# A hybrid decoder layer: the last four down-projection sums seeded into PSUM, two output tiles stored plainly, and a reordered scan

## The chip, the core and the metric

The kernel runs on one NeuronCore of a Trainium2 chip. The metric is the device time of one execution in microseconds (us); lower is better. The kernel before takes 1620.8 us (median of three runs, 1617.77 to 1620.87).

## What is computed

One decoder layer over 1024 tokens (plus 16 meta tokens) of width 1024, in float32:

```python
h = concatenate([meta_tokens, x])
mix = hybrid_mixer(rmsnorm(h, norm_mix_pre), ...)   # attention (8 heads) beside a Mamba-2 SSD scan, then @ w_out
h = h + rmsnorm(mix, norm_mix_post)
f = square(relu(rmsnorm(h, norm_mlp_pre) @ w_mlp_up)) @ w_mlp_down
h = h + rmsnorm(f, norm_mlp_post)
return h[:, N_META:]
```

The change touches three places: attention's transfers, the scan's order of work, and the last two lines, where `f` is normalised over its 1024 columns, weighted and added to the residual `h`.

## The kernel before, in words

Every matrix product is made of three passes in float32r, on operands cut into a high and a low part (high x high, high x low, low x high). The order of each engine's work is written out by hand, one function per engine and phase, with semaphores between them. An engine waits for a semaphore in its own order, so whatever is queued behind a waiting instruction waits too. `SP` (SyncE) issues nearly all transfers and computes nothing; accumulating transfers (`accum_op`) are issued by GpSimd.

**Attention** (`phase_attend`) works head after head. In `on_sync`, `head(h, ...)` issues for each head: the weights of head h+2, two "pieces" (`pieces(h, 0, 2)`), the rotated queries of head h+1 (`rotated`, four transfers, line 1469), a third piece, the first half of the head's output (`outputs(h, 0)`), the remaining pieces and the second half. A piece is a block of scan input that GpSimd weights and cuts in four parts; `store_piece` waits for GpSimd's two results, stores each as two parts (line 1488), and loads the piece after next (line 1481). GpSimd's next piece waits in turn for those stores. TensorE begins head h+1's scores at line 1722, behind a wait for the rotated queries (`a_qr_in`). Scan inputs and attention work share the time of this phase.

**The scan** (`phase_rest`, `chunk(t)` in each engine's function) works through eight chunks of 128 tokens. TensorE mixes the scan's own products with 16 blocks of the output projection, `attention(t, n0, n1)`, each three matmuls of 512 columns. Blocks 0 to 7 make one sum in PSUM bank 4, blocks 8 to 15 another in the same bank, so between block 7 and block 8 ScalarE has to copy the bank out (`mix_out(t, 0)`, line 2873) into `mixs`. TensorE's order in the middle of a chunk t of 1 to 5: blocks 5 and 6; `update(t)` (the state's product, line 2609); `diag(t, 1)` (line 2624); `decays(t, 3)` (lines 1343 and 1344); block 7; `diag(t, 2)`; a wait for the copy; blocks 8 to 11; `diag(t, 3)`; blocks 12 to 15. Chunk 0 has `update` later, and in chunk 6 the first eight blocks of chunk 7 stand before its own blocks 8 to 15. ScalarE's order there: exponentials 2 (`expo(t, 2)`, line 1359), `w_hi(t, 2)` (line 1370), `expo(t, 3)`, `mix_out(t, 0)`, `w_hi(t, 3)`. `expo(t, 3)` waits for `decays(t, 3)`.

**The MLP** runs in slices of 256 hidden columns. For each slice TensorE makes the up products (line 2784) and then 16 down products, two halves for each of eight row tiles, six matmuls of 512 columns each (line 2798; in the last slice line 2833, `down_last`). Each goes to PSUM, and VectorE adds it to the running sum `acc` in SBUF (line 3261, in the last slice `last_add`, line 3458, both halves of a tile in one instruction of 1024 columns). The order of tiles is `TILES`; i below is the place in it, 0 to 7. In the last slice tile i uses the two PSUM banks from `LAST_BANK[i % 4]`, so four tiles fill the eight banks and tile 4 takes the banks of tile 0.

**The end** makes, for each tile, a sum of squares on ScalarE (`last_square`, line 3072, 1024 columns of `acc`), one VectorE instruction (`last_v`, line 484), a square root on ScalarE (`last_sqrt`, line 3077) and five small VectorE instructions (`last_r`, lines 491 to 499), then the scaling by that number and by the weight row `e_wrow` (`last_scale`, line 3470, or, for tiles 2 and 6, ScalarE's line 3082 and GpSimd's multiplication, line 2550; for tile 7 two halves on VectorE, line 3498). `STATS_OF` says which tiles share one set of small instructions: 0; 1, 2; 3, 4; 5, 6; 7. The residual already stands in the output in HBM, and GpSimd issues accumulating stores onto it, one of 512 KB a tile (line 2554) and two of 256 KB for tile 7 (line 2558). SyncE's last wait is for all of them.

The lines that set the end's banks and order:

```python
TILES = [4, 5, 6, 7, 0, 1, 2, 3]
STATS_OF = ((0, 1), (1, 3), (3, 5), (5, 7), (7, 8))
BY_ACT = (2, 6)
LAST_BANK = (2, 4, 6, 0)
```

## Time and profile before

| | |
|---|---|
| median of three runs | 1620.8 us |
| the profiled execution, its own time | 1622.34 us |
| its span, first to last instruction | 1620.5 us |
| granted TensorE clock, mean of the span | 0.995 |
| TensorE busy | 1575.7 us (97%) |
| VectorE, ScalarE, GpSimd busy | 948.6, 599.4, 817.8 us |

The profiled execution is 1.84 us longer than its span and 1.5 us above the median. All places below are us from the start of the span. The phases in it: the input projection to about 360 us, attention to 665, the scan to about 841, the output projection's rest and the first norms to about 950, the MLP to 1602.5, and the end to 1620.5.

In a timeline row the first number is the start, the second the duration, and the bracket at the end is the engine's idle time before the row and what ended it. "x2" means that two instructions are merged in the row. In a window row each engine has its busy time and, in brackets, its count of instructions; then come the granted clock, the DMA engines' busy share and what they moved.

### The profile page before, as it was taken

How to read it: one execution, taken by the hardware profiler on the slowest of the kernel's cores; microseconds unless marked ns; L12 is line 12 of the kernel's file. 1: busy time of each engine (PE TensorE's matmuls, PEld its weight loads, DVE VectorE, ACT ScalarE, POOL GpSimd, SP SyncE). 2: the span in 40 equal slices, each digit the busy share in tenths (PEclk: the TensorE clock that was granted, in tenths of full speed). 3: DMA queues.
4: the chain of work that ended last, by engine and by line, in shares of the span. 5: the costliest groups of instructions: out<-in, count | busy, mean ns of one | idle time of the engine just before them, and what ended most of it. 6: DMA issues, size and time to landing. Idle time of an engine off the chain costs nothing.

```text
span 1620.5 us, 23514 instructions
## 1 busy us (share of the span) xinstructions
PE 1575.7 (97%) x8150; PEld 1353.1 (83%) x8150; DVE 948.6 (59%) x1582; ACT 599.4 (37%) x1149; POOL 817.8 (50%) x775
## 2 busy tenths in 40 slices
PE   7999999999999999899999999999999999999995
PEld 6999998878888888688887888888888888888884
DVE  4756525267677768577778668744444444444446
ACT  5222221245444544455554441433333323322223
POOL 7434453165776558642322340755555555555553
PEclk9999999999999999999999999999999999999998
DMA  6344512235556454788977720111111111111116
GB/s 209 108 139 126 160 56 69 65 109 175 166 147 185 127 155 146 272 312 286 333 245 263 266 79 27 52 52 52 52 52 51 49 50 51 52 52 52 51 46 104
DMA packets 180118, 204.22 MB, mean 126 GB/s; under 512 B 16328, under 2 KB 143152, under 8 KB 180048
## 3 DMA queue, kind: packets, MB, share of 16 engines
q1 hardware_dynamic: 178752, 199.12, 38.3%
q0 software_dynamic: 1296, 4.19, 1.6%
q8 instruction: 41, 0.67, 0.2%
q14 instruction: 29, 0.24, 0.0%
HBM read 133.96 MB, written 69.30 MB: 125 GB/s over the span
## 4 chain that ended last, share of the span: by engine, by line
PE 88%; DMA 3%; POOL 3%; DVE 3%; SPq 1%; issue 1%; ACT 1%; POOLq 0%; DVEq 0%; ACTq 0%
PE ps L2798 17%; PE ps L2784 17%; PE ps L793 7%; PE ps L852 6%; PE ps L2644 6%; PE ps L2719 4%; PE ps L1760 3%; PE ps L2750 3%; PE ps L2764 3%; PE ps L808 2%; PE ps L824 2%; PE ps L1746 2%; PE ps L1729 2%; PE ps L1677 1%; PE ps L2598 1%; PE ps L2833 1%
## 5 line engine op out<-in xcount | busy, mean ns | idle before, releaser
L3261 DVE TENSOR_TENSOR acc<-ps,acc 128x512 f32<-128x512 f32 x208 | 142.4, 690 | 114.8 <-PE ps L2798 114.8
L173 POOL TENSOR_TENSOR ring<-stage,zero 128x512 fp32r<-128x512 f32 (+2 forms) x83 | 91.2, 1099 | 190.9 <-DMA stage<-w_in 48.1
L2798 PE MATMUL ps<-wdlo,fshi 128*128 128x512 f32 x416 | 161.8, 389 | 0.0
L2798 PE MATMUL ps<-wdhi,fshi 128*128 128x512 f32 x416 | 161.8, 389 | 0.0
L2798 PE MATMUL ps<-wdhi,fslo 128*128 128x512 f32 x416 | 161.8, 389 | 0.0
L2534 POOL TENSOR_TENSOR wdlo<-wd_b,wdhi 128x512 fp32r<-128x512 f32 x56 | 70.7, 1293 | 141.4 <-ACT wdhi L3032 141.4
L3289 DVE TENSOR_TENSOR ps<-ps,fs_b 128x512 f32<-128x512 f32 x42 | 29.4, 699 | 150.6 <-PE ps L2784 150.6
L175 POOL TENSOR_TENSOR ring<-stage,ring 128x512 fp32r<-128x512 f32 (+2 forms) x83 | 109.6, 1321 | 6.5
L2644 PE MATMUL ps<-ring,s_aT 128*128 128x512 f32 x384 | 99.6, 403 | 5.9 <-DMA s_aT<-d_attlo 3.2
L793 PE MATMUL ps<-hThi,ring 128*128 128x346 f32 (+1 forms) x480 | 94.4, 325 | 0.0
L3027 ACT ACTIVATE fs_b<-ps 128x512 f32<-128x512 f32 x42 | 25.1, 597 | 184.1 <-PE ps L2784 184.1
L2798 PEld LDWEIGHTS ps<-wdhi,fshi 128*128 128x128 f32 x416 | 78.1, 188 | 16.4
L2798 PEld LDWEIGHTS ps<-wdhi,fslo 128*128 128x128 f32 x416 | 78.1, 188 | 16.2
L2798 PEld LDWEIGHTS ps<-wdlo,fshi 128*128 128x128 f32 x416 | 78.1, 188 | 16.1
L2644 PEld LDWEIGHTS ps<-ring,s_aT 128*128 128x128 f32 x384 | 71.3, 190 | 22.8 <-issue 4.1
L2719 PE MATMUL ps<-ring,s_aT 128*128 128x512 f32 x336 | 80.7, 397 | 1.0 <-DVE ring L3148 0.6
L852 PE MATMUL ps<-hThi,ring 128*128 128x512 f32 x256 | 80.4, 394 | 0.8 <-DVE dt L1119 0.8
L2506 POOL TENSOR_TENSOR wS_b<-wS_b,par 128x512 f32<-128x512 f32 x14 | 14.6, 1041 | 129.0 <-DMA wA_b<-w_mlp_up 129.0
L793 PEld LDWEIGHTS ps<-hThi,ring 128*128 128x128 f32 x480 | 78.7, 189 | 0.2
L2719 PEld LDWEIGHTS ps<-ring,s_aT 128*128 128x128 f32 x336 | 62.2, 188 | 16.4 <-DVE ring L3148 1.2
L2457 POOL TENSOR_TENSOR s_y<-s_y,s_off 128x512 f32<-128x512 f32 x16 | 21.2, 1322 | 103.0 <-DVE s_y L3119 103.0
L1854 ACT ACTIVATE pThi<-ps 128x512 fp32r<-128x512 f32 (+3 forms) x112 | 51.2, 506 | 31.8 <-PE ps L1746 31.8
(500 smaller groups left out, 4591.7 us busy)
## 6 DMA issues: line engine op xcount, KB each, us to landing
wd_b<-w_mlp_down SPq DMA_DIRECT2D x28, 512.0 KB, 3.9
wA_b<-w_mlp_up SPq DMA_DIRECT2D x42, 256.0 KB, 2.8
stage<-w_in SPq DMA_DIRECT2D x40, 256.0 KB, 2.7
stage<-w_out SPq DMA_DIRECT2D x28, 256.0 KB, 5.7
xt<-x SPq DMA_DIRECT2D x8, 512.0 KB, 7.3
d_xT<-xdT SPq DMA_DIRECT2D x8, 512.0 KB, 3.3
d_x<-x_tok SPq DMA_DIRECT2D x8, 512.0 KB, 4.6
d_zT<-zs SPq DMA_DIRECT2D x16, 256.0 KB, 2.3
```

What stands on the lines that cost most here:

```text
L173: pool.tensor_tensor(hi, src, k.zero[:, 0:1].broadcast_to([P, width]), ALU.add).then_inc(k.sem(fam + "_hi"), 1)
L175: pool.tensor_tensor(lo, src, hi.bitcast(F32), ALU.subtract).then_inc(k.sem(fam + "_cut"), 1)
L793: mm = pe.matmul(ps[:, base + q, 0:w], W[a][:, (8 * c + kk) % RING, P * j:P * j + P], hT[b][:, kk, c0:c0 + w], start=(kk == 0 and (a, b) = ...
L852: mm = pe.matmul(ps[:, g % 4, :], W[a][:, (8 * c + kk) % RING, P * j:P * j + P], hT[b][:, kk, c0:c0 + 512], start=(kk == 0 and (a, b) == ( ...
L1760: mm = pe.matmul(ps[:, bank, c0:512], v[a][:, u, vt, :], pT[b][:, j + 1, c0:512], start=(j < 0 and (a, b) == (0, 0)), stop=(j == last and ...
L1854: act.activation(pT[0][:, p0:p0 + np_, P * (b % 4):P * (b % 4) + P], ps[:, turn_bank(b, i, more), 0:P * np_].rearrange("p (a b) -> p a b", ...
L2534: pool.tensor_tensor(half(wd[1][:, j, :], c), half(wd_plain[:, j, :], c), half(wd[0][:, j, :], c).bitcast(F32), ALU.subtract).then_inc(sem ...
L2644: mm = pe.matmul(ps[:, MIX, :], aT[a][:, (t + 1) % 2, kk, :], W[b][:, KD * c + kk, :], start=(nth == 0 and (a, b) == (0, 0)), stop=(nth == ...
L2719: mm = pe.matmul(ps[:, unit_banks(i)[g], :], s[a][:, kk, :], W[b][:, KD * c + kk, :], start=(kk == 4 * g and (a, b) == (0, 0)), stop=(kk = ...
L2784: mm = pe.matmul(bank, mats[q][a][:, kk, :], MOVING[q][b][:, kk, :], start=(fresh and kk == 0 and (a, b) == (0, 0)), stop=(last and kk == ...
L2798: mm = pe.matmul(ps[:, 2 + n % 4, :], fs[a][:, j, P * t:P * t + P], half(wd[b][:, j, :], c), start=(j == 0 and a == 0 and b == 0), stop=(j ...
L3261: dve.tensor_tensor(part, ps[:, 2 + n % 4, :], part, ALU.add).then_inc(sem("v_added"), 1)
```

## The change

- Attention, SyncE: the rotated queries of the next head are issued ahead of pieces 0 and 1 and no longer between them and piece 2.
- Scan, TensorE: in chunks 1 to 6 block 7 stands directly behind block 6, ahead of `update`, `diag(t, 1)` and `decays(t, 3)`. In chunks 0 to 5 block 12 stands ahead of `diag(t, 3)` (in chunk 0 also ahead of `update`). ScalarE: in chunks 1 to 6 `mix_out(t, 0)` stands ahead of `expo(t, 3)`.
- End: for tiles 4 to 7 (`SEEDED`) ScalarE copies the running sum from `acc` into the tile's PSUM banks (`last_seed`), and TensorE's products add onto it, with no `start`. VectorE's `last_add` of these four is gone. ScalarE's squares and VectorE's scaling of them read PSUM.
- End: GpSimd's and ScalarE's part of the scaling of tiles 2 and 6 is gone; VectorE scales tile 2. Tiles 6 and 7 (`PLAIN`) have a set of small instructions each. Their product with the weight row (`last_weighted`) is made before the root is known, and `last_sum` multiplies it by the root and adds the residual, which SyncE has loaded back from the output before. SyncE stores the four halves plainly. GpSimd keeps the accumulating stores of tiles 0 to 5.

```diff
@@ -1510,11 +1510,10 @@
             if left >= 2:
                 sp.wait_ge(sem("a_cut"), 4 * h + 8)
                 head_weights(sp, k, h + 2)
-            pieces(h, 0, 2)
             if left >= 1:
                 sp.wait_ge(sem("a_s"), NT * h + 1)
                 rotated(h + 1, 1 - u)
-            pieces(h, 2, 3)
+            pieces(h, 0, 3)
             outputs(h, 0)
             pieces(h, 3, None)
             if left == 1:
@@ -2127,6 +2126,8 @@
     assert o == o_acc
     e_wrow, _ = m.at("e_wrow", [P, D], F32, slot(0))
     e_junk, _ = m.at("e_junk", [P, D], F32, slot(1))
+    e_h = [m.at(f"e_h{n}", [P, D], F32, slot(2 + n))[0] for n in range(2)]
+    e_w = [m.at(f"e_w{n}", [P, D], F32, slot(4 + n))[0] for n in range(2)]
 
     run, state, sth, es = k.run, k.state, k.sth, k.es
     room4, _ = m.at("w_last", [P, STAGES, 512], F32, O_R)
@@ -2232,10 +2233,21 @@
     RESULTS = ((0, 1, Y, "S2"), (1, 1, V, "S1"), (0, 0, Z, "A11"), (1, 0, X, None))
     KEPT = {q: (j, h) for j, h, _, q in RESULTS}
     TILES = [4, 5, 6, 7, 0, 1, 2, 3]
-    STATS_OF = ((0, 1), (1, 3), (3, 5), (5, 7), (7, 8))
-    BY_ACT = (2, 6)
+    STATS_OF = ((0, 1), (1, 3), (3, 5), (5, 6), (6, 7), (7, 8))
+    SEEDED = NT // 2
+    PLAIN = NT - 2
     LAST_BANK = (2, 4, 6, 0)
     ADDED = 4 + DN
+
+    def last_banks(i):
+        return ps[:, LAST_BANK[i % 4]:LAST_BANK[i % 4] + 2, :]
+
+    def two(x):
+        return x.rearrange("p (c n) -> p c n", c=2)
+
+    def last_sum_in(i):
+
+        return last_banks(i) if i >= SEEDED else two(acc[:, TILES[i], :])
 
     TABLES = ((T2, 5), (T2, 10), (T1, 14), (T3, 15), (T1, 19), (T3, 20), (T4, 23), (T4, 26))
 
@@ -2446,7 +2458,14 @@
         sp.dma_start(e_wrow[:, :], io["norm_mlp_post"][0].partition_broadcast(P)).then_inc(sem("e_w_in"), 16)
         for u in range(2):
             sp.wait_ge(sem(f"m_sent{u}"), 16 * NT // 2)
-        sp.wait_ge(sem("e_sent"), 16 * (NT + 1))
+            sp.dma_start(e_h[u][:, :], rows(io["out"][0], TILES[PLAIN + u])).then_inc(sem(f"m_h_in{u}"), 16)
+        for n in range(4):
+            t, c = TILES[PLAIN + n // 2], n % 2
+            sp.wait_ge(sem("e_half"), n + 1)
+            sp.dma_start(half(rows(io["out"][0], t), c), half(acc[:, t, :], c)).then_inc(sem(f"m_sent{n // 2}"), 16)
+        sp.wait_ge(sem("e_sent"), 16 * PLAIN)
+        for u in range(2):
+            sp.wait_ge(sem(f"m_sent{u}"), 16 * NT // 2 + 32)
 
     def on_gpsimd(pool):
         def gate(t, g):
@@ -2541,21 +2560,9 @@
             down_low(G)
         for u in range(2):
             pool.wait_ge(sem(f"m_sent{u}"), 16 * NT // 2)
-        pool.wait_ge(sem("e_w_in"), 16)
-        for i in range(LAST):
-            t = TILES[i]
-            by_act = sum(n <= i for n in BY_ACT)
-            if i in BY_ACT:
-                pool.wait_ge(sem("e_scl"), by_act)
-                pool.tensor_tensor(acc[:, t, :], acc[:, t, :], e_wrow[:, :], ALU.mult).then_inc(sem("e_out"), 1)
-                pool.wait_ge(sem("e_out"), by_act)
-            else:
-                pool.wait_ge(sem("m_scaled"), NT - len(FUSED) + i + 1 - by_act)
-            pool.dma_start(rows(io["out"][0], t), acc[:, t, :], accum_op=ALU.add).then_inc(sem("e_sent"), 16)
-        for c in range(2):
-            t = TILES[LAST]
-            pool.wait_ge(sem("e_half"), c + 1)
-            pool.dma_start(half(rows(io["out"][0], t), c), half(acc[:, t, :], c), accum_op=ALU.add).then_inc(sem("e_sent"), 16)
+        for i in range(PLAIN):
+            pool.wait_ge(sem("m_scaled"), NT - len(FUSED) + i + 1)
+            pool.dma_start(rows(io["out"][0], TILES[i]), acc[:, TILES[i], :], accum_op=ALU.add).then_inc(sem("e_sent"), 16)
 
     def on_tensor(pe):
         def similar(t):
@@ -2672,23 +2679,24 @@
             attention(t, 3, 5)
             diag(t, 0)
             decays(t, 2)
-            attention(t, 5, 7)
+            attention(t, 5, 8 if t else 7)
             if t:
                 update(t)
             diag(t, 1)
             decays(t, 3)
-            attention(t, 7, 8)
+            if t == 0:
+                attention(t, 7, 8)
             diag(t, 2)
             if t == LAST - 1:
                 attention(LAST, 0, 8)
                 diag(t, 3)
                 attention(t, 8, 16)
             else:
-                attention(t, 8, 12)
+                attention(t, 8, 13)
                 if t == 0:
                     update(t)
                 diag(t, 3)
-                attention(t, 12, 16)
+                attention(t, 13, 16)
 
         def mm_unit(i):
 
@@ -2826,12 +2834,12 @@
                 t = TILES[i]
                 if n in (0, 4, 6):
                     pe.wait_ge(sem("v_sq_out"), 2 + UP + of_sub(G, 4, {0: 2, 4: 3, 6: 4}[n]))
-                if i >= 4 and c == 0:
-                    pe.wait_ge(sem("v_added"), ADDED + of_sub(G, DN, 2 * (i - 4) + 2))
+                if i >= SEEDED and c == 0:
+                    pe.wait_ge(sem("e_seed"), i - SEEDED + 1)
                 for j in range(2):
                     for a, b in PASSES:
                         mm = pe.matmul(ps[:, LAST_BANK[i % 4] + c, :], fs[a][:, j, P * t:P * t + P], half(wd[b][:, j, :], c),
-                                       start=(j == 0 and a == 0 and b == 0), stop=(j == 1 and a == 1))
+                                       start=(i < SEEDED and j == 0 and a == 0 and b == 0), stop=(j == 1 and a == 1), skip_group_check=True)
                 mm.then_inc(sem("v_down"), 1)
 
         down_first()
@@ -2894,10 +2902,12 @@
                 w_cuts(RING + STAGES + 2, RING + KD)
             expo(t, 2)
             w_hi(t, 2)
+            if 0 < t < LAST:
+                mix_out(t, 0)
             expo(t, 3)
             if t == LAST:
                 mix_out(t, 1)
-            else:
+            elif t == 0:
                 mix_out(t, 0)
             w_hi(t, 3)
             if t == 0:
@@ -3064,38 +3074,43 @@
         with act.Fori(FIRST_SUB + 1, SUBS) as G:
             sub(G)
         def last_square(i):
-            act.wait_ge(sem("v_added"), ADDED + of_sub(SUBS - 1, DN, 2 * i + 2))
+            if i < SEEDED:
+                act.wait_ge(sem("v_added"), ADDED + of_sub(SUBS - 1, DN, 2 * i + 2))
+            else:
+                act.wait_ge(sem("v_down"), DN + of_sub(SUBS - 1, DN, 2 * i + 2))
             if i:
                 act.wait_ge(sem("m_sq"), len(STATS) + i)
             else:
                 act.wait_ge(sem("v_up"), UP + of_sub(SUBS, 7))
-            act.activation(e_junk[:, :], acc[:, TILES[i], :], ACT.Square, accum_out=ss[:, i:i + 1]).then_inc(sem("m_sq"), 1)
+            act.activation(two(e_junk), last_sum_in(i), ACT.Square, accum_out=ss[:, i:i + 1]).then_inc(sem("m_sq"), 1)
 
         def last_sqrt(n):
             own = slice(*STATS_OF[n])
             act.wait_ge(sem("m_v"), len(STATS) + n + 1)
             act.activation(s_[:, own], v[:, own], ACT.Sqrt).then_inc(sem("m_sqrt"), 1)
 
-        def last_scale(i):
-            n = [i in range(*x) for x in STATS_OF].index(True)
-            act.wait_ge(sem("m_rs"), 5 * (len(STATS) + n + 1))
-            act.activation(acc[:, TILES[i], :], acc[:, TILES[i], :], ACT.Copy, scale=r[:, i:i + 1]).then_inc(sem("e_scl"), 1)
+        def last_seed(i):
+            act.wait_ge(sem("v_added"), ADDED + of_sub(SUBS - 1, DN, 2 * (i - SEEDED) + 2))
+            act.activation(last_banks(i), two(acc[:, TILES[i], :]), ACT.Copy).then_inc(sem("e_seed"), 1)
 
         last_square(0)
         last_sqrt(0)
+        last_seed(4)
         last_square(1)
+        last_seed(5)
         last_square(2)
         last_sqrt(1)
+        last_seed(6)
         last_square(3)
-        last_scale(2)
+        last_seed(7)
         last_square(4)
         last_sqrt(2)
         last_square(5)
+        last_sqrt(3)
         last_square(6)
-        last_sqrt(3)
+        last_sqrt(4)
         last_square(7)
-        last_scale(6)
-        last_sqrt(4)
+        last_sqrt(5)
 
     def on_vector(dve):
         def mul(t, q):
@@ -3454,8 +3469,8 @@
         up_sub(SUBS - 1)
         def last_add(i):
             dve.wait_ge(sem("v_down"), DN + of_sub(SUBS - 1, DN, 2 * i + 2))
-            part = acc[:, TILES[i], :].rearrange("p (c n) -> p c n", c=2)
-            dve.tensor_tensor(part, ps[:, LAST_BANK[i % 4]:LAST_BANK[i % 4] + 2, :], part, ALU.add).then_inc(sem("v_added"), 2)
+            part = two(acc[:, TILES[i], :])
+            dve.tensor_tensor(part, last_banks(i), part, ALU.add).then_inc(sem("v_added"), 2)
 
         def last_v(n):
             own = slice(*STATS_OF[n])
@@ -3467,7 +3482,19 @@
             rsqrt_after(dve, k, r[:, own], v[:, own], s_[:, own], t_[:, own], "m_sqrt", len(STATS) + n + 1, "m_rs", 5 * (len(STATS) + n))
 
         def last_scale(i):
-            dve.scalar_tensor_tensor(acc[:, TILES[i], :], acc[:, TILES[i], :], r[:, i:i + 1], e_wrow[:, :], ALU.mult, ALU.mult).then_inc(sem("m_scaled"), 1)
+            dve.scalar_tensor_tensor(two(acc[:, TILES[i], :]), last_sum_in(i), r[:, i:i + 1], two(e_wrow), ALU.mult, ALU.mult).then_inc(sem("m_scaled"), 1)
+
+        def last_weighted(u):
+            dve.wait_ge(sem("m_sq"), len(STATS) + PLAIN + u + 1)
+            dve.tensor_tensor(two(e_w[u]), last_sum_in(PLAIN + u), two(e_wrow), ALU.mult).then_inc(sem("m_weighted"), 1)
+
+        def last_sum(u):
+            i = PLAIN + u
+            dve.wait_ge(sem("m_weighted"), len(FUSED) + u + 1)
+            dve.wait_ge(sem(f"m_h_in{u}"), 16 * NT // 2 + 16)
+            for c in range(2):
+                dve.scalar_tensor_tensor(half(acc[:, TILES[i], :], c), half(e_w[u], c), r[:, i:i + 1], half(e_h[u], c),
+                                         ALU.mult, ALU.add).then_inc(sem("e_half"), 1)
 
         last_add(0)
         last_v(0)
@@ -3480,22 +3507,22 @@
         last_v(1)
         last_r(1)
         last_scale(1)
-        last_add(4)
-        last_add(5)
+        last_scale(2)
         last_v(2)
-        last_add(6)
         last_r(2)
         last_scale(3)
         last_scale(4)
         last_v(3)
-        last_add(7)
         last_r(3)
         last_scale(5)
         last_v(4)
+        last_weighted(0)
         last_r(4)
-        for c in range(2):
-            part = half(acc[:, TILES[LAST], :], c)
-            dve.scalar_tensor_tensor(part, part, r[:, LAST:NT], half(e_wrow, c), ALU.mult, ALU.mult).then_inc(sem("e_half"), 1)
+        last_sum(0)
+        last_v(5)
+        last_weighted(1)
+        last_r(5)
+        last_sum(1)
 
     return on_sync, on_gpsimd, on_tensor, on_scalar, on_vector
```

## Rows read from the trace of the kernel before

**Rows 1.** The page: the span and TensorE's busy time.

```profile
span 1620.5 us, 23514 instructions
PE 1575.7 (97%) x8150; PEld 1353.1 (83%) x8150; DVE 948.6 (59%) x1582; ACT 599.4 (37%) x1149; POOL 817.8 (50%) x775
```

**Rows 2.** What TensorE waited for: us in total, times, longest us.

```profile
PE ps L2644 <- ACT mixs L2873: 2.6, 6, 0.4
...
PE ps L1722 <- DMA qr1lo<-d_qrlo: 0.4, 1, 0.4
```

**Rows 3.** Time windows: busy of each engine, granted clock, DMA share, GB/s.

```profile
793.00:815.50 22.50, 22.15 (x124) 18.81 (x124) 16.19 (x25) 11.87 (x28) 7.02 (x5) 1.00 1.03 383
...
1606.00:1618.00 12.00, 0.00 (x0) 0.00 (x0) 6.91 (x12) 2.15 (x4) 5.86 (x5) 0.57 1.05 190
```

**Rows 4.** Timeline of the end, TensorE: the last two products.

```profile
1601.90 0.39 PE L2833 MATMUL ps<-wdlo,fshi 128*128 128x512 f32 x1
1602.13 0.39 PE L2833 MATMUL ps<-wdhi,fslo 128*128 128x512 f32 x1
```

**Rows 5.** Timeline of the end, VectorE.

```profile
1592.88 0.16 DVE L484 TENSOR_SCALAR stat<-stat 128x2 f32<-128x2 f32 x1
1593.32 0.17 DVE L491 RECIPROCAL stat<-stat 128x2 f32<-128x2 f32 x1 [0.27 <-ACT stat L3077]
...
1594.31 1.29 DVE L3470 SCALAR_TENSOR_TENSOR acc<-acc,stat,e_wrow 128x1024 f32<-128x1024 f32 x1
1595.51 1.22 DVE L3458 TENSOR_TENSOR acc<-ps,acc 128x1024 f32<-128x1024 f32 x1
...
1608.44 3.02 DVE L493 TENSOR_TENSOR stat<-stat 128x1 f32<-128x1 f32 x1
...
1612.07 1.42 DVE L3498 SCALAR_TENSOR_TENSOR acc<-acc,stat,e_wrow 128x512 f32<-128x512 f32 x2
```

**Rows 6.** Timeline of the end, GpSimd, and the landing of its last two stores.

```profile
1608.76 2.67 POOL L2550 TENSOR_TENSOR acc<-acc,e_wrow 128x1024 f32<-128x1024 f32 x1
...
1613.12 1.76 POOL L2558 DMA_DIRECT2D out<-acc  x2 [0.53 <-DVE acc L3498]
...
DMA to landing us min/median/max: 5.3/5.7/6.0
```

**Rows 7.** ScalarE: timeline of the end, and the line that exponentiates PSUM.

```profile
1593.19 1.04 ACT L3072 ACTIVATE e_junk<-acc 128x1024 f32<-128x1024 f32 x1
...
1594.31 1.16 ACT L3082 ACTIVATE acc<-acc,stat 128x1024 f32<-128x1024 f32 x1
...
L2885 ACT ACTIVATE eb<-ps x7: 1038/1045/1048, 689.3 to 830.7; 128x1024 f32<-128x1024 f32 x7
```

**Rows 8.** DMA issues of the page: KB each, median us to landing.

```profile
d_zT<-zs SPq DMA_DIRECT2D x16, 256.0 KB, 2.3
```

**Rows 9.** Timeline of one scan chunk, the fourth: ScalarE, TensorE, VectorE.

```profile
744.47 0.60 ACT L1370 ACTIVATE wlhi<-ps 128x512 fp32r<-128x512 f32 x1 [1.16 <-DVE ps L1366]
...
745.71 1.21 DVE L3136 TENSOR_TENSOR state<-ps,state 128x1024 f32<-128x1024 f32 x1
...
746.13 1.14 ACT L1359 ACTIVATE es<-ps,nacum 128x128 f32<-128x128 f32 x4 [1.06 <-PE ps L1344]
...
747.14 0.61 ACT L2873 ACTIVATE mixs<-ps 128x512 f32<-128x512 f32 x1
...
747.90 0.94 PE L2644 MATMUL ps<-ring,s_aT 128*128 128x512 f32 x3 [0.43 <-ACT mixs L2873]
```

**Rows 10.** Timeline of attention's first head, SyncE's queue.

```profile
392.65 1.75 SPq L1469 DMA_DIRECT2D qr1lo<-d_qrlo  x2
...
409.43 0.45 SPq L1481 DMA_DIRECT2D xp_a<-d_x  x1
413.25 0.37 SPq L1475 DMA_DIRECT2D d_atthi<-oThi  x1
```

**Rows 11.** The same head's end on TensorE.

```profile
398.89 0.33 PE L1722 MATMUL ps<-kT1hi,qT1hi 128*128 128x144 f32 x1 [0.38 <-DMA qr1lo<-d_qrlo]
```

## The prediction

> **What bounds the kernel now.** I read the page first. TensorE is busy 1575.7 of 1620.5 us [rows 1], so up to the end of its work only two things can move the time: TensorE's own idle moments, and the tail that is left once it has finished. The waits of TensorE name the first: six of 0.43 us in the scan for ScalarE's copy `mixs` (2.6 us in all), and one of 0.4 us in attention for the rotated queries [rows 2]. The timeline gives the second: the last product starts at 1602.13 and ends at 1602.52 [rows 4], the span at 1620.5, a tail of 18.0 us. The reader is to see there that VectorE ends at 1612.07 + 1.42 = 1613.49 [rows 5], GpSimd issues the last store from 1613.12 + 1.76 - 1.10 = 1613.78 (the longer of the two takes 1.10), and that store lands 6.0 later, at 1619.8 [rows 6]. From there to the end of the span are 0.7 us of final barrier. Meanwhile the DMA engines are full: 1606 to 1618 has a busy share of 1.05 while only 190 GB/s move. The same engines move 383 GB/s at a share of 1.03 with plain transfers [rows 3]. So an accumulating store costs the engines about twice a plain one: 524 KB are 2.76 us at 190 GB/s and 1.37 us at 383. The tail is bound first by VectorE's chain of small steps, then by a queue of accumulating stores.
>
> **Scan.** The wait comes about so: block 7 ends the sum just ahead of `diag(t, 2)`, ScalarE is in its four exponentials until 746.13 + 1.14 = 747.27, the copy starts behind them and takes 0.61, and block 8 starts at 747.90 after 0.43 us of idling [rows 9]. A 512-column product follows another every 0.227 us (1601.90 to 1602.13 [rows 4], in the unrounded mean), a block of three takes 0.68. After the change block 7 stands ahead of `update` (six products) and the sum is complete by 744.3. ScalarE's `w_hi(t, 2)` ends at 744.47 + 0.60 = 745.07 [rows 9], so the copy runs to 745.7, ahead of exponentials that could not start anyway: their input, `decays(t, 3)`, is what ended ScalarE's wait at 746.13 [rows 9], and it comes a block later, at 746.8. Block 8 then follows `diag(t, 2)` at once, at 747.47. What is late next: exponentials 3 end at 747.95 and not 747.27, the low part for `diag(t, 3)` some 0.3 us later than before (the copy no longer stands in between), but `diag(t, 3)` itself stands a block later (0.68), so it is covered. VectorE's state sum waits for `update`, now complete about 745.6, and it began at 745.71 before [rows 9]: not delayed. SyncE's loads behind `update` move by at most 0.7 us and are used a whole chunk later. Gain 6 x 0.43 = 2.6 us; bounds 1 (a new short wait in some chunks) and 2.7. Chunk 0 gets its `update` one block later; its results are used only in chunk 1, I cost it at nothing; if that cover fails it is up to 0.7. TensorE is never far from full afterwards, so the gain passes on to its end.
>
> **Attention.** In the first head the four transfers are issued behind two pieces, the last two from 392.65 to 394.40 [rows 10], and TensorE's scores of the next head start 0.38 late at 398.89 [rows 11]. Issued ahead of those pieces they land several us sooner: gain 0.38. Its condition (the first scores of this head done) is long met, so SyncE does not block. What is moved past: each of seven heads' pieces 0 and 1 go out up to 2.3 us later, and GpSimd's next piece waits for them. The cover is SyncE's idle time ahead of the head's second output half, 409.43 + 0.45 to 413.25 = 3.4 us [rows 10], and that piece 2 no longer has the four transfers ahead of it. I take 0.4, bounds 0 and 0.7.
>
> **End, products.** The six matmuls of a half stay, so TensorE has nothing less to do. It waits for a seed at tiles 4 to 7; a tile is 12 products, 2.72 us, so counted back from 1602.52 tile 4 begins at 1591.6 and tile 7 at 1599.8. No row shows ScalarE writing PSUM from SBUF at this size. The nearest are 1.16 from SBUF to SBUF [rows 7] and 1.05 from PSUM to SBUF [rows 7]; I take 1.1. Each seed's sum is in SBUF a slice earlier and its banks are free after `last_add` of tile i - 4. The worst case is tile 7: seed 6 waits behind a square root until 1593.2 and the chain gives 1593.2 + 1.1 (seed 6) + 1.15 (square 3) + 1.1 (seed 7) = 1596.6, 3.2 us ahead of need. Cost nothing; the cover is that slack.
>
> **End, VectorE.** Its prices: one `last_v` to the first of the five small ones 0.44 (1592.88 to 1593.32), the five 0.99 (to 1594.31), a scaling 1.20 (to 1595.51), two halves 1.42 [rows 5]. A scaling or weighting out of PSUM I put at the same 1.20: the add at 1595.51, which reads PSUM, takes 1.22 [rows 5]. Square 4 ends on ScalarE at 1596.6 + 1.15 = 1597.8 (a square starts to the end of its accumulator 1.15; the reading from PSUM is the same by the 1.05 against 1.04 of rows 7). From there: `last_v` and small ones of tiles 3 and 4, 1.43; two scalings 2.4 (1601.6); the set of tile 5, 1.43, as its root has to wait for `last_v` behind those scalings; scaling 5, 1.2; `last_v` of tile 6, 0.1; its weighting 1.2, under which the root hides; five small ones 0.99; two half sums 1.42; the same 0.1 + 1.2 + 0.99 + 1.42 for tile 7. Sum 1597.8 + 13.9 = 1611.7, against 1613.49: gain 1.8. In this the four adds of 1.2 us are gone (VectorE's share of the tail falls), two scalings came to it, and a stall is gone: the one-column multiplication at 1608.44 took 3.02 and not 0.16, since GpSimd's multiplication ran beside it from 1608.76 for 2.67 [rows 5, 6].
>
> **End, stores.** GpSimd now only issues. By the scalings above, the accumulating store of tile 2 goes out at about 1597 and those of tiles 3 to 5 at 1600.5, 1601.7 and 1604.5. Each keeps the DMA engines 2.76 us; with tile 2's done at about 1603 the three behind it are through about 1611.3. Tile 6's plain halves are issued at 1607.4 and 1608.1 and add 1.4. Tile 7's are issued at 1611.0 and 1611.7. A 256 KB store on a quiet queue lands after 2.3 us [rows 8]; behind a full one the last landed after 6.0 [rows 6]. These are the bounds. The queue should be nearly empty, so I take 2.8: landing at 1614.5, end of the span 0.7 later, 1615.2 to 1615.3. By the Trainium skill ("DMA: Bandwidth & Descriptors", the specifications and the anatomy of a DMA) a 256 KB transfer would take an estimated 2.0 us fixed plus 0.6 at 27 GiB/s on each of 16 engines, 2.6 in all, and the span would end 0.2 earlier. The two loads of the residual (1 MB, 2.7 us at 383 GB/s) stand in SyncE's order behind the load of `e_wrow`, ahead of all of the last slice's down products, over 20 us ahead of use: nothing. Tail: 1620.5 - 1615.3 = 5.2 us gained. Bounds: 1.8 (VectorE's alone, landing as before) and 1.8 + (6.0 - 2.3) = 5.5, with up to 1.0 more if VectorE's waits for ScalarE hide better than I count, 6.5.
>
> **The sum.** 2.6 + 0.4 + 5.2 = 8.2 us. The profiled execution took 1622.34 with a span of 1620.5; it becomes about 1614.1 with a span of 1612.3. It stands 1.5 above the median of the runs, 1620.8, so the median becomes 1612.6.
>
> **Rivals.**
> 1. The plain stores share the DMA engines with what is left of the accumulating ones. For it: the share was 1.05 up to the end, and four accumulating stores need 11 us from 1600.5 on. Against: the first of tile 7's halves goes out when my account has them through. It decides if VectorE's chain ends ahead of 1611 or the stores run later than I count. Then the last store lands 5 to 6 us after its issue and the tail gives 1.8 to 2.8, in all 5.3: 1615.5. The Trainium skill says ("DMA: Bandwidth & Descriptors", "Issuing engines are not separate DMA queues") that transfers of all issuing engines run on the same 16 engines and interleave; if so a plain store can't pass the backlog.
> 2. The scan gives nothing: the same copy or exponentials, moved by 0.7 us, make TensorE wait elsewhere (ahead of `diag(t, 3)` or in the next chunk's `along`, which needs the state). For it: ScalarE and VectorE work in long in-order chains. Against: the times above leave 0.4 to 1.6 us. Total 5.6: 1615.2. With rival 1 together 2.7: 1618.1, which is no change.
> 3. Slower. Place: attention's SyncE queue. Four transfers of 256 KB ahead of pieces 0 and 1 delay GpSimd's pieces by their issue (2.3) plus a slower landing, and if that is more than the 3.4 us of idle time per head, GpSimd cuts the next head's weights late and TensorE waits in each head. At a delay of 5.2, 1.8 x 7 heads = 12.6 us: 1620.8 - 8.2 + 12.6 = 1625.2. Against: in the code the weights are cut nearly a head ahead of use, and the four transfers were in the same head before.
> 4. The change doesn't do what it says: the products replace the seeds. Then the output is another, but no instruction takes another time, so this has no price of its own.
>
> **Chances and range.** Forecast 0.72; rival 1 0.10; rival 2 0.09; both 0.05; rival 3 0.04. A change of 0.2% (3.2 us) is about what a measurement can tell from none. Faster: forecast, 1 and 2 with part of their spreads, 0.86; same: both, and the edges, 0.10; slower 0.04. For the range: from all upper bounds (2.7 + 0.7 + 6.5 = 9.9, 1610.9) with 1.5 for the spread of the three runs, 1609.4, to rivals 1 and 2 with the same spread, 1617.0.
>
> **What would show it.** Right: TensorE's waits no longer name `mixs`, and none of the scan's is over 0.2 us; `L1722` no longer waits for `qr1`; the last product starts 3.0 us earlier, at 1599.1; VectorE ends 9.2 us after the last product and not 11.0; no small instruction of VectorE takes 3 us; the last store lands within 3 us of its issue; from the last product's end to the span's end it is 12.8 us and not 18.0. Wrong: a wait of TensorE for the seeds, a busy share over 1 of the DMA engines at the last landing, a new wait in the scan, or waits for cut weights in attention.

## The result and the profile after

The changed kernel takes **1607.68 us** (median of five runs, 1606.19 to 1611.63) against 1619.17 for the kernel before, timed beside it. The ratio of the two is 0.9938, 95% interval [0.9923, 0.9952]; of 1619.17 that is a gain of 10.0 us, 7.8 to 12.5. The ratios below are meant so too, each against the kernel before timed beside it. A repeat (below) gave 0.9944 [0.9931, 0.9958], 9.1 us. The forecast was 1612.6, 0.9949 of its base, within both intervals; but the time itself lies 1.7 us below the low end of the range, 1609.4. The profiled execution took 1607.61 with a span of 1605.8, the one of before 1622.34 and 1620.5.

The page of the changed kernel [rows 1]:

```profile
span 1605.8 us, 23522 instructions
PE 1572.6 (98%) x8150; PEld 1352.0 (84%) x8150; DVE 944.7 (59%) x1589; ACT 600.6 (37%) x1152; POOL 811.8 (51%) x770
```

TensorE's waits in it (us in total, times, longest) [rows 2]. The six for `mixs` have become one, but that one is long, and there is none for the rotated queries:

```profile
PE ps L1721 <- ACT prob L1859: 2.1, 2, 1.4
...
PE ps L2651 <- ACT mixs L2881: 1.1, 1, 1.1
...
PE ps L2651 <- DMA s_aT<-d_attlo: 0.8, 1, 0.8
```

Its end, the timeline of TensorE [rows 4]:

```profile
1592.12 0.39 PE L2841 MATMUL ps<-wdhi,fslo 128*128 128x512 f32 x1
```

of VectorE [rows 5]:

```profile
1587.24 0.17 DVE L484 TENSOR_SCALAR stat<-stat 128x2 f32<-128x2 f32 x1 [0.46 <-ACT e_junk L3085]
...
1588.69 1.28 DVE L3485 SCALAR_TENSOR_TENSOR acc<-acc,stat,e_wrow 128x1024 f32<-128x1024 f32 x1
1589.89 1.27 DVE L3485 SCALAR_TENSOR_TENSOR acc<-ps,stat,e_wrow 128x1024 f32<-128x1024 f32 x1
...
1597.21 1.21 DVE L3489 TENSOR_TENSOR e_w<-ps,e_wrow 128x1024 f32<-128x1024 f32 x1
...
1599.30 1.42 DVE L3496 SCALAR_TENSOR_TENSOR acc<-e_w,stat,e_h 128x512 f32<-128x512 f32 x2
```

of ScalarE, a seed and a square out of PSUM [rows 7]:

```profile
1585.17 1.00 ACT L3094 ACTIVATE ps<-acc 128x1024 f32<-128x1024 f32 x1
1586.12 1.00 ACT L3085 ACTIVATE e_junk<-ps 128x1024 f32<-128x1024 f32 x1
```

and the four plain stores, first their issues, then us from issue to landing (least, median, most) [rows 6]:

```profile
1596.60 4.48 SPq L2465 DMA_DIRECT2D out<-acc  x4
```

```profile
DMA to landing us min/median/max: 3.7/5.2/6.8
```

The end in windows [rows 3]; the last two figures are the DMA engines' busy share and GB/s:

```profile
1590.00:1596.00 6.00, 2.51 (x12) 1.74 (x10) 5.38 (x16) 2.41 (x6) 2.58 (x3) 0.91 1.09 195
1596.00:1602.00 6.00, 0.00 (x0) 0.00 (x0) 4.54 (x11) 0.20 (x1) 0.00 (x0) 0.50 1.00 221
```

Read together: the last product ends at 1592.51. Before the root of tiles 3 and 4, VectorE waits 0.46 for square 4, and from then on it hardly pauses. Its scaling takes as long from PSUM as from SBUF (1.27 and 1.28), and no small instruction takes 3 us any more. It ends at 1599.30 + 1.42 = 1600.72, 8.2 us after the last product. The DMA engines are full up to 1602, at 195 and 221 GB/s: the accumulating stores are not through when the plain ones come. The last lands at 1605.3, 4.6 after VectorE's end.

Between the two traces lie 14.8 us, more than the 10.0 that the times give. By stretch: the start up to the first projection product 1.9 less; from there to the first scores 1.0; from the first scores to the scan 2.7; from the scan to the last product's end 4.4 (937.3 to 932.9); the tail 4.8. Nothing was changed ahead of the scores, and over all traces of this study, of either kind, the first of these places lies anywhere from 45.6 to 48.0 us (before 47.55, after 45.64). So these 2.9 are not the change's, and some of the rest is chance too: the trace of before has 3.41 us at half clock at the scan's start (from 665.7), which that of after has not there. I therefore repeated both kernels and read each stretch in many traces.

### The profile page after: what moved, and what is told of

It reads as the page before. It is cut to its first block, busy times and chain, and to the rows that moved or that the text cites. A ratio compares the mean times of both kernels' runs of the same rounds, so it can differ in the third digit from the quotient of the medians.

```text
span 1605.8 us, 23522 instructions
## 1 busy us (share of the span) xinstructions
PE 1572.6 (98%) x8150; PEld 1352.0 (84%) x8150; DVE 944.7 (59%) x1589; ACT 600.6 (37%) x1152; POOL 811.8 (51%) x770
## 4 chain that ended last, share of the span: by engine, by line
PE 89%; DVE 3%; DMA 2%; POOL 2%; SPq 1%; issue 1%; ACT 1%; DVEq 0%; POOLq 0%; ACTq 0%
PE ps L2806 18%; PE ps L2792 17%; PE ps L793 7%; PE ps L852 6%; PE ps L2651 5%; PE ps L2727 4%; PE ps L1759 3%; PE ps L2758 3%; PE ps L2772 3%; PE ps L808 2%; PE ps L824 2%; PE ps L1745 2%; PE ps L1728 2%; PE ps L1676 2%; PE ps L2605 1%; PE ps L1698 1%
```

## The experiments

### Both kernels again

The kernel before, with no edit:

> The kernel before, unchanged, for a second trace of it. Open is how much of the 10.0 us by which the products ended sooner in the changed kernel's trace (1602.5 to 1592.5) is the change at all: 1.9 of it stand at the first input product (47.6 to 45.6), where nothing was changed. Theory A, the first transfers' landing varies from execution to execution: the first input product starts somewhere between 45 and 48 here as well, and the scan's start (665.2 before) moves with it and by a few us more, for TensorE's wait for the attention output was 3.2 us in one trace and 0.8 in the other. Theory B, the change makes it: this trace has 47.6, 665.2 and 3.2 within 0.3. The ratio is 1.000 under both.

Ratio 1.0006 [0.9996, 1.0016], its span 1617.9 against 1620.5: the trace from which I predicted was a long one.

The changed kernel, with no edit:

> The changed kernel, unchanged, for more runs and a second trace. The parts alone gave 0.9983 (scan), 0.9955 (end) and 1.000 (attention), product 0.9938, which is the ratio first measured. Theory: 0.994 again, the median near 1610, and a trace in which the scan's chunks 1 to 5 are 21.94 long, the wait in chunk 6 is about 1.1, VectorE ends 8.2 after the last product and the span ends 12 to 13.5 after it; its start and the wait at the scan's start differ from the first trace by up to 3 us. Rival: the parts help one another beyond their sum (the first median, 11.5 below the median of before), and the ratio is 0.993 or less.

0.9944 [0.9931, 0.9958], 1608.6 us. The last product ends at 1594.03, 5.7 ahead of the 1599.75 of the other repeat; in the first pair of traces it was 10.0. The tail, from the last product's end to the end of the span, is 12.3 us here, 13.3 in the first trace. The wait in chunk 6 is there again.

### The three parts alone

```diff
-            pieces(h, 0, 2)
             if left >= 1:
                 sp.wait_ge(sem("a_s"), NT * h + 1)
                 rotated(h + 1, 1 - u)
-            pieces(h, 2, 3)
+            pieces(h, 0, 3)
```

> The change of attention's SyncE order alone (rotated queries ahead of pieces 0 and 1). The prediction: the wait of 0.38 at the second head goes, nothing else, ratio 0.9997. Rival (theory B): the earlier landing also shortens the wait at the scan's start from 3.2 to about 0.8 and the head starts before it by 1.1, together about 4 us, ratio 0.9975.

> Attention's SyncE order alone, once more. In five traces of the old order the stretch from the first to the second head's scores is 31.3, 31.7, 31.8, 33.1 and (a piece later still) 35.1 us, in all traces of the new order 30.2. Theory: the step is worth 1.1 to 2.9 us, mean 1.8, ratio 0.9989, and this trace has 30.2 again. Rival: what the step gains there is lost by the scan's start (the first timing gave 1.000 with an interval of 0.001 to either side), ratio 1.000.

1.000 [0.999, 1.0011] and 1.0004 [0.9995, 1.0014]: alone, the moved queries show no gain in the time, and the second interval leaves out the 1.8 us that was expected of it.

```diff
-            attention(t, 5, 7)
+            attention(t, 5, 8 if t else 7)
...
-                attention(t, 8, 12)
+                attention(t, 8, 13)
...
+            if 0 < t < LAST:
+                mix_out(t, 0)
             expo(t, 3)
```

> The scan's new order alone. The prediction: six waits of 0.43 go, 2.6 us. The trace of the changed kernel shows 0.64 a chunk in chunks 1 to 5 and a new wait of 1.1 in chunk 6, which leaves 5 x 0.64 - 0.4 = 2.8 us. Theory: a chunk's length falls from 22.58 to 21.94, for besides the wait one separate run of block 7 between two other kinds of product has gone, and each such change of kind costs about 0.1; the wait in chunk 6 is there too, because the store of the first half of mixs (which ScalarE must wait for before it writes the half again) now lies behind four loads. Rival: the 0.64 needs the earlier start that the other parts give, and here a chunk gains only 0.43. Ratio 0.9982 under the theory.

0.9983 [0.9973, 0.9993], 2.8 us. The waits of TensorE keep one row for `mixs`, of 1.19 us, in chunk 6.

The end alone is the changed kernel with those two edits undone:

```diff
-            pieces(h, 0, 3)
+            pieces(h, 2, 3)
...
-                attention(t, 8, 13)
+                attention(t, 8, 12)
```

> The end's part alone: seeds, plain stores of tiles 6 and 7, VectorE scaling tile 2. From the last product to the span's end 18.0 us before, predicted 12.8, 13.3 in the changed kernel's trace. Theory: 13.3 again, the same chain, ratio 1 - 4.7/1620 = 0.9971. Rival: part of the tail's gain came from work of the other parts, and it gains less than 4.

> The end's part alone, once more. The traces give 18.0 to 18.7 from the last product to the span's end before and 12.1 to 13.3 after, a gain of 5.6, where the first timing gave 7.3 with an interval of 4.8 to 9.7. Theory: 5.6, ratio 0.9965, tail in this trace 12 to 13.3. Rival: 7 or more, so that the end's part helps at another place too.

0.9955 [0.994, 0.9971] and 0.9969 [0.9958, 0.9979], 7.3 and 5.0 us. In the traces the tail is 12.1 and 12.8. With the old end it is 18.0 to 18.7 in nine traces, 18.26 in the mean; with the new end 12.1 to 13.3 in seven, 12.63 in the mean. The part is worth 5.6 us, which lies in both intervals. And the moved queries together with the scan, both diffs above:

```diff
-            pieces(h, 0, 2)
...
-                attention(t, 8, 12)
+                attention(t, 8, 13)
```

> The scan's and attention's parts together, without the end's. Theory: the parts add, 3.1 us from the scan (5 chunks by 0.64, less the new wait of chunk 6) and 1.8 from attention, ratio 0.9970; the tail is 18.0 to 18.7 as before. Rival: attention's part adds nothing to the scan's, ratio 0.9982.

0.9971 [0.996, 0.9982], 4.7 us, against 2.8 for the scan alone; the intervals overlap.

### Scan: what a wait is worth, and the new one

A gain of 6 x 0.43 less the new 1.1 would be 1.5 us. The traces show more: of chunks 1 to 5 one with the old order lasts 22.59 us, with the new one 21.94, 0.64 less. Timeline of the kernel before, block 7 and behind it the first product of `diag`, ahead of the wait in [rows 9]:

```profile
745.93 0.86 PE L2644 MATMUL ps<-ring,s_aT 128*128 128x512 f32 x3
...
746.62 0.28 PE L2624 MATMUL ps<-wlhi,xdt_hi 128*128 128x256 f32 x1
```

The same `diag` of the changed kernel, first and last product, and the blocks behind it:

```profile
742.42 0.28 PE L2631 MATMUL ps<-wlhi,xdt_hi 128*128 128x256 f32 x1
...
743.01 0.28 PE L2631 MATMUL ps<-wlhi,xdt_lo 128*128 128x256 f32 x1
743.13 2.26 PE L2651 MATMUL ps<-ring,s_aT 128*128 128x512 f32 x9
```

From the first product of `diag` to the start of block 8 it was 747.90 - 746.62 = 1.28, now 743.13 - 742.42 = 0.71. The wait costs **0.57**, not the 0.43 in its brackets: a product's row is 0.28 long, but the next one can start after 0.12, and the bracket counts only from the row's end. The other 0.07 stand directly behind the wait: the three products of block 8 take 0.94 there [rows 9], those of block 7 take 0.86. So all of the 0.64 is the wait's. The thought, put down ahead of the scan's own run, that changing from one kind of product to another costs 0.1 each time, falls: here `diag` passes to a block at its ordinary pitch.

The new wait, in chunk 6 of the changed kernel. Timelines of TensorE, ScalarE and SyncE:

```profile
812.29 2.10 PE L2651 MATMUL ps<-ring,s_aT 128*128 128x512 f32 x8 [1.08 <-ACT mixs L2881]
```

```profile
811.55 0.60 ACT L2881 ACTIVATE mixs<-ps 128x512 f32<-128x512 f32 x1 [3.87 <-DMA d_mix<-mixs]
```

```profile
804.43 8.06 SPq L2311 DMA_DIRECT2D d_mix<-mixs  x2
```

and a window of the same kernel, with the DMA engines' share and GB/s last:

```profile
782.00:805.00 23.00, 23.00 (x134) 19.72 (x133) 17.36 (x27) 12.65 (x32) 7.10 (x5) 1.00 1.03 385
```

ScalarE has room for its copy only once the store of the half before it has landed. SyncE issues that store at 804.43, behind loads for the next chunk, with the DMA engines at a share of 1.03 up to 805, and it lands at 811.5 (its row merges two stores, of which the second is issued after the copy). The old order asked for the copy later than that. In the seven traces with the new scan order and this store at its old place the wait is 0.7 to 1.8. To test this cause, SyncE stores the half first, in chunk 6 only:

```diff
                 load_z(t)
+                if t == LAST - 1:
+                    store_mix(t, 0)
                 sp.wait_ge(sem("s_sq"), 2 * t)
...
-            store_mix(t, 0)
+            if t != LAST - 1:
+                store_mix(t, 0)
```

> The changed kernel, with one step moved: in chunk 6 SyncE stores the first half of mixs ahead of the loads of the skip input and of the B rows, not behind them. Theory on the new wait of 1.1 in the scan (ScalarE's second copy into that half waits for the store's landing, which stands behind four loads on full DMA engines): the store lands before 809 on the first trace's scale, the wait falls to the 0.4 that the copy itself costs or less, 0.7 to 1.1 us gained, ratio to the changed kernel 0.9995. Rival: the copy is late for another reason (ScalarE's own order), and the wait stays 1.1.

> The changed kernel with the earlier store of mixs in chunk 6, once more, beside the run before it on the same chip. Theory: no wait in chunk 6 of the scan in this trace either, chunk 6 is 1.0 us shorter than in the changed kernel's traces (27.8 against 28.8), the span ends 12.3 to 13.3 after the last product, ratio 0.994. Rival: the wait comes back when the store lands late, as in 1 of 2 traces.

The wait is gone in both traces. Chunk 6, from its first product of `along` to that of chunk 7, takes 28.54 us and not 29.55 or 29.71 as in the two traces of the changed kernel (29.19 in the kernel before), and from the scan to the last product's end it is 931.7 and 932.2 against 932.9. The cause is shown. The times are 0.994 [0.9926, 0.9953] and 0.9931 [0.9918, 0.9945], which can't tell 1 us from nothing.

### Attention: where the gain of the moved queries goes

First the other direction, the queries behind all three pieces:

```diff
-            pieces(h, 0, 2)
+            pieces(h, 0, 3)
             if left >= 1:
                 sp.wait_ge(sem("a_s"), NT * h + 1)
                 rotated(h + 1, 1 - u)
-            pieces(h, 2, 3)
```

> The kernel before, with the rotated queries issued behind three pieces and not two: the opposite of the change's step. The wait for them at the second head was 0.4, 1.4, 0.7 and 2.7 us in four traces of the old order and none in two of the new. Theory: the landing of those four transfers decides that wait, with the head's start as the deadline; issued some 3 us later the wait is 3 to 6 us at the second head, and a wait of 0.5 to 3 appears at later heads too, in all 4 to 12 us slower, ratio 1.0025 to 1.007. Rival: the wait is something else's (the landing slows with the pieces' traffic however they are ordered), and it stays within 0.4 to 2.7, ratio 1.000.

1.0163 [1.0149, 1.0177], 26 us slower, where 4 to 12 were expected. TensorE's waits:

```profile
PE ps L1721 <- DMA qr0lo<-d_qrlo: 13.4, 3, 4.6
...
PE ps L1721 <- DMA qr1lo<-d_qrlo: 5.8, 2, 4.8
```

19 us of waits, and an estimated 12 at most from five stretches of 3.4 to 6.8 us at half clock behind them (half of their 23.9), are enough for it. The old order stands at the edge of this: its traces have 0.4 to 2.7 us of waits for the queries in the first head, with a second wait of up to 0.8 in some, and the stretch from the first head's scores to the second's takes 31.3 to 33.1 us. With the moved queries it is 30.1 to 30.4 in twelve traces and 30.7 in one.

Then why is the time not lower? In the last head, the timelines of TensorE of three kernels. The scan's order alone, queries not moved:

```profile
633.90 0.47 PE L1722 MATMUL ps<-kT1hi,qT1hi 128*128 128x512 f32 x1 [0.66 <-ACT prob L1860]
```

The changed kernel:

```profile
631.52 0.46 PE L1721 MATMUL ps<-kT1hi,qT1hi 128*128 128x512 f32 x1 [1.40 <-ACT prob L1859]
```

Scan and moved queries, GpSimd, ScalarE and TensorE; in the windows the figure behind the five engines is the granted clock, as a share of 2.4 GHz:

```profile
630.40 1.89 POOL L1643 TENSOR_TENSOR es<-s_z,dend 16x1024 f32<-16x1024 f32 x1
632.38 1.05 ACT L1903 ACTIVATE xdt_hi<-es 16x1024 fp32r<-16x1024 f32 x1 [5.63 <-POOL es L1643]
...
634.63 0.77 PE L1721 MATMUL ps<-kT1hi,qT1hi 128*128 128x512 f32 x1 [3.95 <-ACT prob L1859]
```

```profile
630.00:633.00 3.00, 0.68 (x6) 0.36 (x3) 0.00 (x0) 0.62 (x1) 2.29 (x2) 0.97 1.03 311
633.00:636.40 3.40, 1.77 (x5) 1.30 (x6) 2.08 (x6) 2.32 (x7) 2.88 (x2) 0.50 0.60 202
636.40:639.80 3.40, 3.40 (x11) 2.39 (x9) 2.57 (x6) 0.81 (x2) 3.17 (x4) 0.50 0.03 7
```

What holds TensorE is ScalarE, which stands at its copy of the state's start (`xdt_hi`, line 1903) until GpSimd's `es` (line 1643) is there, and that comes at the end of GpSimd's chain of pieces and weight blocks. From the first scores, `es` starts after 263.2 to 264.6 us in the old order (268.3 in the trace that had lost most in the first head) and after 262.6 to 263.1 in the new one: in the mean GpSimd gained 0.8 us where TensorE gained 1.1 or more, so TensorE waits longer for it: 0.7 to 1.4 us in the old order, 1.40 in nine traces of the new. In two of eleven traces with moved queries (the one above and the one with tile 1 stored plainly) GpSimd was 2 us late; these two have the wait of 3.95 and 10.2 us at half clock, and from the first scores to the scan they took 300.3 and 299.6 us, where the other nine took 294.9 to 296.2 (mean 295.4) and the old order 296.0 to 297.6 (mean 296.9), or 302.4 in one of five. Their own times are the highest of their kernels', 1618.95 and 1613.01.

To take that hold away, ScalarE's copy was put behind the exponentials of block 3, in the kernel with moved queries alone and in the kernel before:

```diff
         def scan_start(b):
...
             if b == 3:
+                act.wait_ge(sem("p_xw"), 1)
+                act.activation(k.xh0[0][0:META, :], xwm, ACT.Copy).then_inc(sem("p_xwhi"), 1)
...
-            if b == 2:
-                act.wait_ge(sem("p_xw"), 1)
-                act.activation(k.xh0[0][0:META, :], xwm, ACT.Copy).then_inc(sem("p_xwhi"), 1)
```

> Only the rotated queries of attention are moved (as in the two runs of them alone, 1.000 and 1.0004), and in the last head ScalarE's copy of the state's start, which waits for GpSimd's es, stands behind the exponentials of block 3 and not ahead of them. In the traces with the moved queries this copy holds TensorE for 1.40 us, in two of eleven for 3.95 with about 10 us at half clock. Theory that the gain of the moved queries (1.1 us or more in the first head) is given back at this hold, since GpSimd's chain has not become shorter: no wait for the probabilities over 0.5 us in the last head, no half clock there, from the first head to the scan 292.5 to 294.5 us (295.6 with the hold, 300 in the two), and a ratio to the kernel before of 0.9975 to 0.9990, clearly lower than that of the same edit without the moved queries. Rival, the moved queries gain nothing anywhere and the hold costs nothing: 1.000. Rival, GpSimd is the bound of the last head's end: the wait moves to the products of the state's start, and the ratio stays at 1.000.

> The kernel before with the copy of the state's start behind the exponentials of block 3 of the last head, nothing else. Theory: the hold of 0.66 to 1.40 us in its traces is gone (less than one moved-queries hold), the waits for the rotated queries in the first head stay (0.4 to 2.7), ratio 0.9985 to 0.9997, span from the first head to the scan 295.5 to 297.0. The difference to the run with the moved queries is what these gain once nothing gives it back: 1 to 2 us. Rival that moved queries gain nothing: both ratios are equal.

0.9999 [0.999, 1.0008] and 1.0019 [1.001, 1.0028]. The waits of TensorE in the first of them:

```profile
PE ps L2642 <- DMA s_aT<-d_attlo: 2.7, 1, 2.7
...
PE ps L1779 <- POOL xdt_lo L1645: 0.7, 1, 0.7
```

The wait of 1.40 is gone, but 0.7 comes back one step later at GpSimd's own low part, and at the scan's first block, which waits for the last head's output to come back, it is 2.7 and not the 1.1 and 1.6 of the moved queries alone. From the first scores to the scan it takes 296.0, no less than with the hold. The theory that the hold alone gives the gain back fails: it is one of several waits in a row, and the others end with GpSimd's instructions or SyncE's transfers. Yet between these two kernels the moved queries are worth 0.0020, 3.2 us, with 0.0009 to either side on both ratios, where they gave nothing in the other pair. Why the copy moved alone makes the kernel 3 us slower its trace doesn't show (span 1617.4). What the moved queries bring stays open between 0 and 3 us.

All together, early store and late copy in the changed kernel:

```diff
+                if t == LAST - 1:
+                    store_mix(t, 0)
...
             if b == 3:
+                act.wait_ge(sem("p_xw"), 1)
```

> The changed kernel with the early store of the mixer's half in chunk 6 and the copy of the state's start behind the exponentials of block 3 of the last head. Theory: 1.5 to 3 us below the changed kernel (0.9938, 0.9944) and the one with the early store (0.994, 0.9931): ratio 0.9915 to 0.9930, 1605 to 1606.5 us, no wait of TensorE over 0.5 us for the probabilities in the last head. Rival: the wait moves elsewhere in the last head, 0.993 to 0.994.

0.9946 [0.9932, 0.9959]. Nothing gained; the expectation was wrong.

### The end: what the stores and the seeds are worth

The changed kernel without its plain stores; the seeds stay and GpSimd stores all eight tiles with accumulation:

```diff
-        for i in range(PLAIN):
+        for i in range(LAST):
             pool.wait_ge(sem("m_scaled"), NT - len(FUSED) + i + 1)
...
-        last_weighted(0)
         last_r(4)
-        last_sum(0)
+        last_scale(6)
```

> The changed kernel without its plain stores: VectorE scales tiles 6 and 7 out of PSUM, no residual is loaded back, GpSimd issues accumulating stores for all eight tiles. It splits the end's gain. VectorE's chain is two half-tile steps shorter and ends 6.6 after the last product (8.2 in the changed kernel, 11.0 before); the last store lands 6 us after its issue, as before. Theory A (stores and chain weigh the same): the span ends 13.6 after the last product, so most of the gain of the end is the seeds' and the missing GpSimd multiplications', and the plain stores are worth 0 to 1.5 us. Rival B: eight accumulating stores of 2.76 us each keep the DMA engines busy to 14 us after the last product or later, the span ends 15 to 16 after it, and the plain stores are worth 2 to 3 us.

0.9965 [0.9952, 0.9979]. The DMA engines in windows, busy share and GB/s last:

```profile
1596.00:1602.00 6.00, 0.00 (x0) 0.00 (x0) 2.98 (x9) 0.20 (x1) 2.60 (x3) 0.50 1.06 206
1602.00:1608.00 6.00, 0.00 (x0) 0.00 (x0) 0.00 (x0) 0.00 (x0) 0.00 (x0) 0.50 0.80 150
```

VectorE is done 6.55 us after the last product (8.2 with the plain stores, which cost it the sums with the residual), but the last store lands 8.0 later, and the tail is 15.35. Against 12.63 the plain stores are worth 2.7 us, by one trace, and the seeds with VectorE's shorter chain the other 2.9. What of these 2.9 is the seeds' own is not shown. GpSimd's multiplications went too, and with them VectorE's stall of 3.02 - 0.16 = 2.9 us ahead of the last tile [rows 5, 6]; no run keeps one without the other. The backlog itself was measured in one execution that leaves out the accumulating stores of tiles 3 to 5, whose rows then keep the residual alone:

```diff
-        for i in range(PLAIN):
+        for i in range(3):
```

> The changed kernel without the accumulating stores of tiles 3, 4 and 5 (their rows of the output keep the residual alone). Theory: the last plain stores land late (3.3 to 4.6 us after their issue in three traces) because the DMA engines are still at the accumulating stores; with three of them gone the engines are idle by then and each 256 KB store lands 2.3 to 2.6 us after its issue, and the span ends 11.0 to 11.5 after the last product and not 12.1 to 13.3. Rival: the end of the time is not the backlog's, and they land after 3.3 us or more as before.

From issue to landing (least, median, most) of the four plain stores:

```profile
DMA to landing us min/median/max: 2.0/2.0/2.1
```

It was 3.7/5.2/6.8 in the changed kernel. So rival 1 of the prediction was in part true: SyncE's plain stores land later because of accumulating ones that GpSimd issued. The Trainium skill says ("DMA: Bandwidth & Descriptors", "Issuing engines are not separate DMA queues") that transfers of all issuing engines run on the same 16 engines and interleave. The two medians, 5.2 with the three stores and 2.0 without, agree with that. The 2.0 is less than the 2.3 of [rows 8] and than the 2.6 that the prediction estimated from the Trainium skill. Without the backlog the tail is 10.75; that one execution took 1608.13.

Two attempts to shrink the backlog, on the changed kernel with tile 1's residual added by GpSimd, and on the one with the early store with tile 5 stored plainly too:

```diff
+            if i == 1:
+                pool.wait_ge(sem("m_mix_in0"), 16 * NT // 2 + 16)
+                pool.tensor_tensor(acc[:, TILES[1], :], acc[:, TILES[1], :], e_one[:, :], ALU.add).then_inc(sem("m_turned"), 1)
+                continue
```

> The changed kernel, with tile 1's residual loaded back and added by GpSimd (2.7 us) and the tile stored plainly. Theory: the last plain stores land 3.4 to 4.6 us after their issue and not 2.3 because the accumulating stores keep the DMA engines full (share 1.09 and 1.00 at 195 and 221 GB/s in the first trace); one accumulating store less takes 1.4 us of their work away, and the last landing comes up to 1.4 us sooner, less up to 0.5 us by which GpSimd's addition holds a small VectorE instruction. Rival: the landing is slow for its own reasons, and nothing is gained or 0.5 lost.

```diff
-    PLAIN = NT - 2
+    PLAIN = NT - 3
```

> A candidate for a faster version: the changed kernel with the earlier store of mixs in chunk 6, and tile 5 weighted, summed with its reloaded residual and stored plainly like tiles 6 and 7. Theory (the end is the DMA engines' throughput: a plain tile takes them 1.4 us less than an accumulating one, and 256 KB land 2.1 us after issue on idle engines): VectorE's chain grows by 1.1 us to end 9.3 after the last product, the last stores land 2.1 to 2.8 after their issue, and the span ends 12.0 to 12.6 after the last product, 0.3 to 0.8 sooner than the mean of the changed kernel. Rival: VectorE's 1.1 us weighs more than the shorter queue, and the span ends 12.8 or later.

0.9946 [0.9933, 0.996] and 0.9931 [0.9918, 0.9945]. The first makes VectorE's end 1.6 us later, where up to 0.5 was expected, and the tail 13.88; its timelines of GpSimd and VectorE say how:

```profile
1590.47 3.36 POOL L2572 TENSOR_TENSOR acc<-acc,e_one 128x1024 f32<-128x1024 f32 x1 [4.29 <-DVE acc L3494]
```

```profile
1592.04 1.82 DVE L484 TENSOR_SCALAR stat<-stat 128x2 f32<-128x2 f32 x1 [0.47 <-ACT e_junk L3094]
```

The small instruction of VectorE that runs beside GpSimd's addition takes 1.82 us in place of 0.17 and ends where the addition does: the same event as in the kernel before at 1608.44 [rows 5, 6]. With three plain tiles the last store lands 3.1 after VectorE's end and not 3.4 to 4.6, but VectorE ends 9.1 after the last product and not 8.2: the two cancel, tail 12.66. Neither beats the changed kernel by more than the intervals.

## Why the prediction was right or wrong

**Direction and mechanisms** were right: both waits and the tail that it named were there, and shrank or went. The times of the parts (2.8 for the scan, 5.0 and 7.3 for the end) are near its terms of 2.6 and 5.2. What failed is the size of terms: the base, the price of a scan wait, attention's 0.4 and the landing of the last stores. The time is 4.9 below the forecast: 1.6 is the base, 1.8 the gain (10.0 by the ratio for 8.2), and 1.5 is that the two medians lie 11.5 apart where the ratio gives 10.0.

**Base.** "It stands 1.5 above the median of the runs, 1620.8, so the median becomes 1612.6." The median of three runs was itself 1.6 above the 1619.2 of five. The sign "the last product starts 3.0 us earlier" rested on one trace in the same way: it came 10.0 earlier in the first pair of traces and 5.7 in the second.

**Scan.** "Gain 6 x 0.43 = 2.6 us; bounds 1 and 2.7": two steps failed and nearly cancelled. The price of a wait was read from the brackets, 0.43, and is 0.57 by starts, 0.64 with the slower product behind it: 3.8 us for six. And "none of the scan's is over 0.2 us" was wrong: I followed the copy's inputs (the sum, the exponentials) but not the buffer that it writes, which waits for a store on SyncE; 1.0 us went there. That the sum came near is luck. From the scan's start to the last product's end, over the traces without a stretch at half clock in it, 935.75 became 932.9: 2.85 us.

**Attention.** "gain 0.38 ... I take 0.4, bounds 0 and 0.7" sized the term by one trace, and one that waited little. In five traces of the old order the first head took 31.3 to 33.1 us and with the moved queries mostly 30.2, which is 1.1 to 2.9. From the first scores to the scan the means differ by 1.4, and in the times it is between 0 and 3. The cover ("SyncE's idle time ... 3.4 us") held, so rival 3 did not come: no head waits for cut weights. The prediction did not ask what is late next once TensorE is ahead: GpSimd's chain, 260 us later, in the last head.

**End, products.** "Cost nothing": right, no wait for a seed. A seed took 1.00 to 1.01 and not 1.1, a square from PSUM 1.00.

**End, VectorE.** "Sum 1597.8 + 13.9 = 1611.7": 9.2 us after the last product, measured 8.2. Square 4 was done 5.3 us ahead of the last product's end and not 4.7, thanks to the faster seeds and squares, and the chain took 1600.72 - 1587.24 = 13.5. The 3 us stall went as forecast.

**End, stores.** "The queue should be nearly empty, so I take 2.8": wrong, 3.4 to 4.6, since the backlog was not through ("through about 1611.3", that is 8.8 after the last product; the accumulating store issued last landed at 1603.3, 10.8 after it). The prediction's own numbers say as much: with the 1.4 of tile 6's halves the engines are busy to 1612.7, and tile 7's halves are issued at 1611.0 and 1611.7. The tail is 12.63 in the mean of seven traces against 12.8 forecast, gain 5.6 and not 5.2. That too is in part luck: VectorE's end came 1.0 sooner than forecast, the landing 1.2 later (4.0 in the mean for 2.8), and the final barrier took 0.5 for 0.7.

**Sum and range.** 2.85 + 5.6 and between 0 and 3 for attention make 8.5 to 11.5 us where the forecast had 8.2, and 10.0 and 9.1 were timed. The range's low end was 1620.8 - 9.9 - 1.5. The timed gain used up the 9.9, for the bounds of scan and attention (2.7 and 0.7) were too tight, and the base alone used up the 1.5; what the time lies below is the 1.5 by which the medians are further apart than the ratio says.
